# One-core streaming encoder step: the mLSTM mixer's states in shared tiles, its gate exponentials, table loads and first output projections in another order

## The reference

```
proj = xm @ w_in                       # q, k (8 heads x 64), v, o (8 heads x 128), gates
b = cumsum(lf);  inter = b + m
m_t = max(inter, max_s(b_t - b_s + ig_s))
s = (q k^T) * exp(dmat - m_t)
num = exp(inter - m_t) * (q C) + s v;  den likewise with n
h = num / max(|den|, exp(-m_t))
C_new = exp(b_end + m - m_new) * C + sum_s w_new k v     # n_new and m_new alike
y = (rms(h) * head_g * sigmoid(o)) @ w_out
```

## Time and profile before

| | us |
|---|---|
| median of 3 runs | 1637.97 |
| lowest and highest | 1634.97, 1638.21 |
| the profiled execution's own time | 1638.21 |
| its span, first to last instruction | 1636.4 |

### The profile page before, as it was taken

The page is one execution under the profiler, slowest core; times in us unless marked ns, Lnnn a source line. Parts: engine busy times, 40 slices in busy tenths (PEclk is TensorE's granted clock), DMA queues, the critical chain, the costliest instruction groups (busy, mean ns, idle before and its releaser), DMA issues.

```text
span 1636.4 us, 30939 instructions
## 1 busy us (share of the span) xinstructions
PE 1559.4 (95%) x11910; PEld 1459.1 (89%) x11910; DVE 707.8 (43%) x1266; ACT 366.2 (22%) x857; POOL 759.6 (46%) x440
## 2 busy tenths in 40 slices
PE   5899999999999999999999997888999999999999
PEld 2798899899999999999988795656899999999998
DVE  4602354453343123436865056787454442144421
ACT  2210555321110001112221022676321110011100
POOL 2744423344455544546544443144355555455553
PEclk9899999999999999999999998899899999999999
DMA  9255322444445334443322253121122222222231
GB/s 348 76 176 171 111 79 92 131 139 141 147 141 166 119 108 147 140 164 125 104 78 64 77 196 115 54 74 35 39 85 82 77 89 87 70 89 77 83 116 65
DMA packets 53474, 183.18 MB, mean 112 GB/s; under 512 B 6184, under 2 KB 8624, under 8 KB 53024
## 3 DMA queue, kind: packets, MB, share of 16 engines
q1 hardware_dynamic: 50688, 174.60, 32.5%
q10 hardware_dynamic: 2720, 7.66, 1.2%
HBM read 171.69 MB, written 10.55 MB: 111 GB/s over the span
## 4 chain that ended last, share of the span: by engine, by line
PE 86%; DVE 4%; ACT 2%; issue 2%; POOL 1%; DMA 1%; ACTq 0%; DVEq 0%; SPq 0%; POOLq 0%
PE psum L538 67%; PE psum L586 7%; PE psum L548 3%; PE psum L915 1%; DVE act_lo L1411 1%; PE psum L958 1%; PE psum L818 1%; PE psum L902 1%; PE psum L559 1%; PE psum L685 1%; DMA raw<-in_w_stream 1%; PE psum L930 1%; PE psum L838 1%; PE psum L715 1%; ACT sc L1270 1%
## 5 line engine op out<-in xcount | busy, mean ns | idle before, releaser
L463 POOL TENSOR_SCALAR w_hi<-raw 128x1024 fp32r<-128x1024 f32 (+1 forms) x185 | 212.1, 1147 | 756.1 <-PE psum L538 616.1
L465 POOL TENSOR_TENSOR w_lo<-raw,w_hi 128x1024 fp32r<-128x1024 f32 (+1 forms) x185 | 488.2, 2639 | 15.4
L538 PE MATMUL psum<-act_hi,w_hi 128*128 128x288 f32 x2160 | 478.7, 303 | 16.5 <-DVE act_lo L1480 8.6
L538 PE MATMUL psum<-act_lo,w_hi 128*128 128x288 f32 x2160 | 468.0, 298 | 0.0
L538 PE MATMUL psum<-act_hi,w_lo 128*128 128x288 f32 x2160 | 468.0, 298 | 0.0
L538 PEld LDWEIGHTS psum<-act_hi,w_hi 128*128 128x128 f32 x2160 | 350.4, 191 | 34.9 <-issue 25.3
L538 PEld LDWEIGHTS psum<-act_hi,w_lo 128*128 128x128 f32 x2160 | 352.2, 190 | 0.0
L538 PEld LDWEIGHTS psum<-act_lo,w_hi 128*128 128x128 f32 x2160 | 351.4, 190 | 0.0
L538 PE MATMUL psum<-hid_hi,w_hi 128*128 128x288 f32 x704 | 151.1, 296 | 0.0
L538 PE MATMUL psum<-hid_hi,w_lo 128*128 128x288 f32 x704 | 150.8, 296 | 0.0
L538 PE MATMUL psum<-hid_lo,w_hi 128*128 128x288 f32 x704 | 150.7, 296 | 0.0
(11 more groups left out here) (249 smaller groups left out, 1670.9 us busy)
## 6 DMA issues: line engine op xcount, KB each, us to landing
raw<-in_w_stream SPq DMA_DIRECT2D x153, 512.0 KB, 3.7
ada_ring<-in_ada_w SPq DMA_DIRECT2D x80, 512.0 KB, 3.7
raw<-in_w_down SPq DMA_DIRECT2D x32, 704.0 KB, 4.1
ada_first<-in_ada_w SPq DMA_DIRECT2D x8, 1024.0 KB, 15.3
line_rep<-line SPq DMA_DIRECT2D x8, 352.0 KB, 4.5
line<-line_rep SPq DMA_DIRECT2D x8, 352.0 KB, 5.2
x<-in_x SPq DMA_DIRECT2D x1, 2304.0 KB, 12.2
dec<-line SPq DMA_DIRECT2D x8, 288.0 KB, 4.0
```

What stands on the lines that cost most here:

```text
L463: pool.tensor_scalar(hi, src, 1.0, 0.0, ALU.mult, ALU.add).then_inc(hi_split, 1)
L465: pool.tensor_tensor(lo, src, hi.bitcast(F32), ALU.subtract).then_inc(lo_split, 1)
L538: last = mm(psum[:, b + half, 0:n_cols], w_parts[s][wp][:, k, :], parts[ap][:, k, half * HT:half * HT + n_cols], start=(k == 0 and n == 0) ...
```

## The change

Both heads' states now share tiles: `c0n` and `cp_sb` are [128, 4, 129], the three `c_sb` tiles hold two states each (six places, used in turns), and `core_values` multiplies over the 64 partitions of its head. So VectorE's ten operations a head pair become five, the memsets and the semaphore `c_zero` go, and the eight stores of the states become six.

```
-        c0n = new("c0n", [P, 4, 2, 129])
+        c0n, cp_sb = new("c0n", [P, 4, 129]), new("cp_sb", [P, 4, 129])
-        c_sb = [at(f"c_sb{n}", [P, 2, 129], tail_at[n]) for n in range(3)]
+        c_sb = [at(f"c_sb{n}", [P, 2, 130], tail_at[n]) for n in range(3)]
 # SyncE, load of the given state
-                if a == 0:
-                    sp.wait_ge(c_zero, 1)
-                sp.dma_start(c0n[a * DK:(a + 1) * DK, :, a, :], c0n_in[:, a::2, :]).then_inc(c0n_loaded, 16)
+                sp.dma_start(c0n[a * DK:(a + 1) * DK], c0n_in[:, a::2, :]).then_inc(c0n_loaded, 16)
 # SyncE, load_rows(0)
                     sp.wait_ge(rows_stored, 32)
-                    sp.dma_start(m_out, row(R_MU, TP - 1)).then_inc(m_stored, 16)
 # GpSimd, start
-            for tile in c_sb:
-                pool.memset(tile[:, :, :], 0.0)
-            pool.memset(c0n[:, :, :, :], 0.0).then_inc(c_zero, 1)
 # TensorE, behind the values
+            wait_evac(pe, U_O)
+            wait_evac(pe, U_O + 1)
             ada_turn(30)
-            wait_evac(pe, U_O)
 # TensorE, core_values
-                a, p = h % 2, h // 2
+                o, p = DK * (h % 2), h // 2
+                    c = c0n[o:o + DK, p, :] if j == 4 else c_sb[(3 * (p % 2) + j - 1) // 2][o:o + DK, (3 * (p % 2) + j - 1) % 2, 0:129] if j else None
-                        mm(out_tile(j), qw[:, p, j * P:j * P + n], c_sb[j - 1][:, a, :] if j < 4 else c0n[:, p, a, :], start=True, stop=False)
+                        mm(out_tile(j), qw[o:o + DK, p, j * P:j * P + n], c, start=True, stop=False)
 # TensorE, output projection
-            project(U_OUT + 1, 0, act[1], k1=2)
+            project(U_OUT + 1, 0, act[1], ready=(lo_ready[A_HN], 1), k1=KT - 1)
             ada_turn(39)
             project(U_OUT, 0, act[1], ready=(lo_ready[A_HN], 1), k0=KT - 1)
-            project(U_OUT + 1, 0, act[1], k0=2)
+            project(U_OUT + 1, 0, act[1], k0=KT - 1)
 # ScalarE, loop over units 1 to 8 (m = 0 to 7)
                 if m == 1:
                     sa.wait_ge(lam_dot, 1)
-                    af(lam4[:, 2:4], lam4[:, 0:2], ACT.Exp).then_inc(lam_exp, 1)
                 if m >= 1:
                     ada_out(15 + m)
-                if m == 3:
-                    sa.wait_ge(rows_ready, 1)
-                    steps(af(row(R_W, P), row(R_W, P), ACT.Exp))
-                    af(row(R_FLOOR), row(R_MU), ACT.Exp, scale=-1.0).then_inc(floor_ready, 1)
-                    sa.dma_start(line_dram[:, 1, 0:T], row(R_NEG)).then_inc(rows_stored, 16)
-                    steps.wait()
-                    sa.dma_start(line_dram[:, 2, P:T], row(R_W, P)).then_inc(rows_stored, 16)
+            af(lam4[:, 2:4], lam4[:, 0:2], ACT.Exp).then_inc(lam_exp, 1)
+
+            sa.wait_ge(rows_ready, 1)
+            sa.dma_start(m_out, row(R_MU, TP - 1)).then_inc(m_stored, 16)
+            steps(af(row(R_W, P), row(R_W, P), ACT.Exp))
+            af(row(R_FLOOR), row(R_MU), ACT.Exp, scale=-1.0).then_inc(floor_ready, 1)
+            sa.dma_start(line_dram[:, 1, 0:T], row(R_NEG)).then_inc(rows_stored, 16)
+            steps.wait()
+            sa.dma_start(line_dram[:, 2, P:T], row(R_W, P)).then_inc(rows_stored, 16)
 # ScalarE, values of the second half (VectorE alike): one order of tiles for both halves
-                for tt in (0, 1, 4) if nh == 0 else (4, 0, 1):
+                for tt in (0, 1, 4):
 # ScalarE, core
             def core_guess(h):
+                sa.preload_act_table(ACT.Abs_reciprocal_sqrt)
                 sa.wait_ge(z_ready, h + 1)
                 af(y5, z5, ACT.Abs_reciprocal_sqrt).then_inc(fy_ready, 1)
+                sa.preload_act_table(ACT.Sigmoid)
 ...
-                    if h < H:
-                        sa.preload_act_table(ACT.Sigmoid)
...
-                    sa.preload_act_table(ACT.Abs_reciprocal_sqrt)
 ...
+                        sa.dma_start(cp_out.rearrange("d (p a e) -> d p a e", a=2, e=129)[:, :, a, :], cp_sb[r, :, :]).then_inc(state_stored, 16)
                         for n in range(2):
-                            sa.dma_start(cp_out.rearrange("d (p a e) -> d p a e", a=2, e=129)[:, 2 * n:2 * n + 2, a, :],
-                                         cp_sb[n][r, :, :]).then_inc(state_stored, 16)
 # VectorE, core_state(p)
-                halves2 = [(a, slice(a * DK, (a + 1) * DK)) for a in range(2)]
+                c = lambda j: c_sb[(3 * (p % 2) + j - 1) // 2][:, (3 * (p % 2) + j - 1) % 2, 0:129] if j < 4 else cp_sb[:, p, :]
...
+                steps(ve.tensor_copy(c(1), add(0)))
...
+                for j in range(1, 4):
+                    steps.wait(but=1 if j == 1 else 0)
+                    last = stt(out=c(j + 1), in0=c(j), scalar=keep[:, p, j - 1:j], in1=add(j), op0=ALU.mult, op1=ALU.add)
```

More of the change, by code:

```diff
@@ L268, in build @@
             sem(n) for n in ("absf_ready", "log_ready", "rows_ready", "floor_ready", "c0n_loaded", "m_stored"))
-        c_zero = sem("c_zero")
         rows_stored, dec_masked, dec_ready, qw_ready = (
@@ L304, in build @@
         wend = tmp[0:H, 4, 40:44]
-        cp_sb = [at("cp_sb", [P, 2, 129], tail_at[3]), tmp[:, 3, 184:442].rearrange("p (q e) -> p q e", q=2)]
         pbuf, sg = tmp[:, 0:2, :], tmp[:, 4:6, :]
@@ L393, in _ @@
             load_pairs(U_O, 19, 30)
-            sp.wait_ge(state_stored, 128)
+            sp.wait_ge(state_stored, 96)
             def spread_line(step):
@@ L490, in _ @@
             split_pairs(3, 26)
-            pool.wait_ge(state_stored, 128)
+            pool.wait_ge(state_stored, 96)
             for u0, pairs in ((55, 4), (63, 11), (85, 4), (93, 13)):
@@ L1074, in mixer_values @@
                         last.then_inc(evac[0], 2)
-                    elif tt == 4:
-                        last.then_inc(v_tail, 1)
+                last.then_inc(v_tail, 1)
             def decay(g):
@@ L1132, in _ @@
                         sa.wait_ge(m_stored, 16)
-                    if h < H:
-                        sa.preload_act_table(ACT.Sigmoid)
                     gated_hi(h - 1)
-                else:
-                    sa.preload_act_table(ACT.Sigmoid)
                 if h < H:
@@ L1344, in _ @@
             sa.wait_ge(m_stored, 16)
-            sa.wait_ge(state_stored, 128)
+            sa.wait_ge(state_stored, 96)
             sa.wait_ge(y_stored, 16 * KT)
@@ L1520, in mixer_values @@
                 ve.wait_ge(unit_done, U_V + 4 * nh + 4)
-                for tt in (2, 3) if nh == 0 else (3, 2):
+                for tt in (2, 3):
                     last = ve.tensor_copy(vm[:, tt, 4 * nh:4 * nh + 4, 0:P], psum[:, tt, :].rearrange("p (h e) -> p h e", h=4))
@@ L1621, in core_state @@
                 ve.wait_ge(state_mm, p + 1)
-                halves2 = [(a, slice(a * DK, (a + 1) * DK)) for a in range(2)]
+                c = lambda j: c_sb[(3 * (p % 2) + j - 1) // 2][:, (3 * (p % 2) + j - 1) % 2, 0:129] if j < 4 else cp_sb[:, p, :]
                 add = lambda j: psum[:, 3, TS + 129 * j:TS + 129 * j + 129] if j < 3 else psum[:, 4, P:P + 129]
-                for a, r in halves2:
-                    steps(ve.tensor_copy(c_sb[0][r, a, :], add(0)[r]))
+                steps(ve.tensor_copy(c(1), add(0)))
                 if p == 0:
                     ve.wait_ge(c0n_loaded, 32)
-                for a, r in halves2:
-                    steps(stt(out=cs_sb[p // 2][r, p % 2, :], in0=c0n[r, p, a, :], scalar=keep[r, p, 3:4], in1=psum[r, 4, P + 129:P + 258],
-                              op0=ALU.mult, op1=ALU.add))
+                steps(stt(out=cs_sb[p // 2][:, p % 2, :], in0=c0n[:, p, :], scalar=keep[:, p, 3:4], in1=psum[:, 4, P + 129:P + 258],
+                          op0=ALU.mult, op1=ALU.add))
                 for j in range(1, 4):
[L1632 to L1637, removed]
+                    steps.wait(but=1 if j == 1 else 0)
+                    last = stt(out=c(j + 1), in0=c(j), scalar=keep[:, p, j - 1:j], in1=add(j), op0=ALU.mult, op1=ALU.add)
+                    if j < 3:
+                        steps(last)
                 last.then_inc(state_out, 1)
@@ L1672, in _ @@
             modulation(40, 48, [], 4)
-            ve.wait_ge(state_stored, 128)
             norm_rstd(N_FFN0)
```

## The result

| | us |
|---|---|
| before | 1638.1, median of 4 (1634.97 to 1641.13) |
| after | 1657.6, median of 4 (1654.94 to 1658.87) |
| ratio | 1.0117, 95% interval 1.0094 to 1.014 |
| forecast | 1645.5 (1640.8 to 1650.0), slower 0.84 |

What follows compares the result with a forecast made beforehand. TensorE was taken to bound the kernel; from 1638.0 us, waits of 2.3 + 0.2 + 0.3 + 0.2 + 2.5 = 5.5 plus 2.0 for the clock gave 1645.5 us, range 1640.8 to 1650.

Steps and rivals of the forecast that it cites:

- the state products on 64 partitions: TensorE, L714 in the core: 64 instructions read 64 partitions, columns unchanged; +0.3 us, at most +1.6, low end -7.0.
- The gate section: Gate exponentials behind unit 8's eviction: TensorE's values start 2.3 us later, between +1.8 and +3.6.
- the issue of m's store: Ahead of the gate exponentials, with the lambda exponential: adds 0.45 us, bounded by 0 and 0.75.
- VectorE's small operations: VectorE's `ends` behind the gate exponentials: 0.25 us for its 1.25 us operation, 1.1 in all, 2.09 at the other end.
- The split of unit 10: GpSimd's split, its load behind stores and row loads: starts near 124, ready at 127.5; 0.2 us counted, 0 to 1.5.
- The output order: Units 25 and 26 reordered: GpSimd splits unit 27 late, TensorE idles 2.5 us before it, between 2.0 and 3.0.
- The table loads: ScalarE, around the guess: 1.28 us each, scaling 1.42 later; 0 for heads 0 to 6, bare on head 7.
- case (c): Rival: a table switch occupies ScalarE about twice its row's length, delaying the core's transposes; 1654.5 us, chance 0.03.
- The end of the core: Head 7, ahead of the last transposes: table load 1.42 less 1.2 from six stores, +0.2 us, up to +1.4.
- The clock: TensorE's clock falls: 3.0 us each, even chances at two new idle places, one in three that the present goes; +2.0.

Runs made afterwards that it cites:

- the second time: The changed kernel run once more, unchanged, against before: 1657.1 us, ratio 1.0104 (1.0088 to 1.012).
- the grouped kernel: Changed kernel with a head's four state products issued in a row, then its five value products: 1654.8 us, ratio 1.0093 to before.

## Why the prediction was right and wrong

**The term that failed: the state products on 64 partitions.** I took +0.3 us, between -7.0 and +1.6. They cost 10.5, and the time came out 7.6 us above the upper end of my range. Of the nine products of a head, five followed their neighbour at 0.22 us and now at 0.42; the other four, the first of the head and those at tile 4, go from 0.27 to 0.33 up to 0.36 to 0.42. That is 1.3 us a head, 10.5 in eight. The mistake was in my bounds, which came from the length of one product and its columns. What the step changes is not a product's length but whether its weight load may start beside the product ahead of it, and the earlier trace rows priced a product inside a run of equal ones. The trace of before did hold places that hint at the price. For tile 4 the weights go from 128 to 64 columns, and there, too, the load starts only with its product, 0.32 us after the last one instead of 0.22. And behind the scores, over 64 partitions, the first load of the projection, over 128, starts with its product at 225.17, while the next starts 0.13 us ahead of its own at 225.54:

```profile
222.71 0.39 PE L714 MATMUL psum<-c_sb,qw 128*128 128x129 f32 x2
222.93 0.39 PE L715 MATMUL psum<-vm,tmp 128*128 128x129 f32 x2
223.25 0.43 PE L714 MATMUL psum<-c0n,qw 128*64 128x129 f32 x2
...
223.25 0.19 PEld L714 LDWEIGHTS psum<-c0n,qw 128*64 128x64 f32 x2
...
225.17 0.30 PEld L538 LDWEIGHTS psum<-act_hi,w_hi 128*128 128x128 f32 x2
225.41 0.32 PEld L538 LDWEIGHTS psum<-act_lo,w_hi 128*128 128x128 f32 x2
```

From these rows an estimate of the upper bound would have been 0.1 us or more for each of 64 changes, 6.4 us and up, instead of 1.6.

The Trainium skill (TensorE: Matmul & The Clock Gate, LDWEIGHTS (loading the stationary operand)) was right in what I took from it: 64 and 128 partitions load in the same time, 0.29 and 0.30 us in the rows. The Trainium skill, in the section "Step-by-step: what each phase is for" of the same page, says that a load is pulled ahead when its row groups don't conflict or it goes into the background buffer. In the rows a load over 128 partitions starts while a product over 128 still runs, and no load starts ahead where 64 partitions meet 128 (or 64 columns meet 128). That section does not set this case apart; the measurement decides.

**The gate section** was right in mechanism, short in size: 2.3 forecast, 3.7 measured (12.47 for 8.73). The term that was short is the issue of m's store. I took 0.45 us for it, at most 0.75, from 0.54 on SyncE's queue; on ScalarE's it took 1.84 and 2.05, and behind the short lambda exponential, which ran during the issue, ScalarE began nothing before its end. Without that store the gap was 1.52 us. VectorE's small operations were short, 0.18 us for 1.25, as I took it. The split of unit 10 began at 127.43, not near 124. Of these 3.4 us 1.4 is the later start of unit 8, 1.3 the longer issue of m's store, 1.0 the issue of one row load (1.50 us for 0.47) and 0.5 the landing, less 0.7 by which the two stores landed sooner than I took. The split ended at 130.96, 1.1 us before TensorE came to it, only because unit 9 had become 1.5 us slower; that no wait came here was luck.

**The output order**: 2.5 forecast, 2.44 measured. **The table loads**: right; the rows have the guess directly behind a load and no further time, so case (c) falls. By my number, 1654.5, (c) was the rival nearest to the measured 1657.6, but its mechanism was not there. The load's price where nothing covers it is 4.14 - 2.57 = 1.57, near my 1.42:

```profile
301.43 1.28 ACT L1108 ACT_TABLE_LOAD   x1
302.72 0.21 ACT L1110 ACTIVATE tiny<-tiny 128x5 f32<-128x5 f32 x1
302.95 1.28 ACT L1111 ACT_TABLE_LOAD   x1
```

**The end of the core.** After waits 1.35 us there, less than before: TensorE comes 1.3 us later and the chain over ScalarE does not. That gives 1.2 of the 10.5 back.

**The clock** sums to +0.1 in after's profile, where I had +2.0: +1.5 at unit 9, +1.5 at unit 27, -2.9 behind the values. A fall costs 1.5 to 2.9 there, and 1.3 to 4.7 over all profiles (unit 9 at 8.47 for 7.13, V at 23.60 for 18.9), not 3.0 everywhere. The chances were off too. Over fourteen profiles, the first values unit was slow in all seven with the late gate section (8.47 to 9.91 us) and in none of the others; unit 27 in three of six with the 2.4 us gap; unit 17 in nine of twelve with the gap of 1.4 to 1.5 us (V 22 to 23.6, or 19) and in one of two with 0.7, and the place behind the last transposes in five, twice with before's own gap of 2.6 us. So that a place did not fall in one profile was weak evidence.

**The start.** Unit 1 starts 1.5 us later in after's profile. In eight kernels with before's start code it lies between 56.42 and 58.23, in six with after's between 57.05 and 58.06. The spans overlap; the change is not shown to be its cause.

**The sum.** The parts alone on before, by ratio: 0.45% (64 partitions), 0.22% (gate), 0.26% (output), 0.06% (tables), together 0.99%, against 1.04% and 1.17% for after; each has an interval of about 0.2% to either side, so that they agree so closely is in part luck. In after's profile the core brings 9.3, gate and output 3.7 + 2.5 of waits, the start and units 1 to 7 1.4, the clock 0.1: 16.9. What the medians have beyond it (19.5 here, 17.0 the second time) lies within the scatter of single times, 1635.0 to 1646.2 for before over all rounds, and isn't put down to a place. With the right first term the forecast would have been 1645.5 + 10.2 - 1.2 = 1654.5.

## What to carry to other kernels

A change that leaves the number and columns of TensorE's products alone can still slow them: look at whether neighbours cover the same partitions, and price a change of height from a place in the trace where one occurs, not from a product inside a run. Halving the partitions that a product reads bought nothing here and cost up to 0.2 us at each change; keep the zero halves, or group by height (a head's nine products took 2.35 us over 128 partitions, 2.68 grouped, 3.65 mixed; the grouped kernel did not add the two parts up). A small store belongs on a queue that is waiting anyway: moving eight of them from ScalarE to SyncE took 2.6 us off the path, while moving them along ScalarE's own queue only moved the gap.

## What was not expected of the hardware

- Between a product over 128 and one over 64 partitions, in either order, the next starts after 0.42 us instead of 0.22 (129 columns, f32, full clock, runs of 128 columns of weights), and its weight load starts with it instead of 0.11 us ahead.
- The issue of one small store took 1.76 to 2.05 us on ScalarE's queue in six profiles, 0.36 and 0.54 on SyncE's, and ScalarE computed nothing in the last 1.5 to 1.7 us of it. Why it took so long is open; the next two stores there took 0.28 each, and single issues on SyncE's queue were long too (a row load at 1.35 and 1.50 us for 0.47).
- The same gap of 1.4 to 1.5 us ahead of the same work cost nothing by the clock in three profiles and 2.9 us or more in nine.
